# Feed-forward groups of a float32 decoder trunk: loads, sums, products and out units in another order

## The reference

```python
def _swiglu(x, w_in, w_out):
    gate, up = jnp.split(x @ w_in, 2, axis=-1)
    return (jax.nn.silu(gate) * up) @ w_out

x = x + 0.5 * _rmsnorm(_swiglu(_rmsnorm(x, ng[0]), ffn1_w_in[i], ffn1_w_out[i]), ng[1])
```

## Time and profile before

| | us |
|---|---|
| median of 3 runs | 2258.42 (2258.36 to 2259.06) |
| profiled execution | 2256.88 |
| its span, first to last instruction | 2255.2 |
| TensorE busy | 2199.7 (98%) |
| VectorE busy | 1549.6 (69%) |
| ScalarE busy | 1139.2 (51%) |
| GpSimd busy | 366.1 (16%) |

### The profile page before, as it was taken

How to read it: one execution, slowest core, us unless ns; L and a number is a source line. 1 busy time by engine, 2 the same in 40 slices (tenths; PEclk the granted TensorE clock), 3 DMA queues, 4 the chain that set the end, 5 groups by cost and what they waited for, 6 DMA issues and landing times.

```text
span 2255.2 us, 30953 instructions
## 1 busy us (share of the span) xinstructions
PE 2199.7 (98%) x11642; PEld 1819.9 (81%) x11642; DVE 1549.6 (69%) x1942; ACT 1139.2 (51%) x1639; POOL 366.1 (16%) x287
## 2 busy tenths in 40 slices
PE   9999999999999999999999999999999999999999
PEld 7788788788787887888787887787778888778787
DVE  6989536777568996358888338877666735888723
ACT  5445434655555455345445436567566734544422
POOL 2031000100111120001212001021822110121200
PEclk9999999999999999999999999999999999999999
DMA  5322332222223323333331332222212132532241
GB/s 169 124 82 78 108 96 86 83 78 85 65 90 112 112 75 91 96 94 107 117 113 52 97 95 88 85 75 66 66 48 85 57 94 72 143 131 94 92 133 66
DMA packets 84767, 208.59 MB, mean 92 GB/s; under 512 B 25088, under 2 KB 29312, under 8 KB 84640
## 3 DMA queue, kind: packets, MB, share of 16 engines
q1 hardware_dynamic: 84112, 206.59, 29.4%
q10 hardware_dynamic: 528, 0.26, 0.0%
HBM read 202.56 MB, written 4.26 MB: 92 GB/s over the span
## 4 chain that ended last, share of the span: by engine, by line
PE 78%; DVE 10%; issue 5%; ACT 3%; POOL 2%; DMA 2%; SPq 0%; DVEq 0%; ACTq 0%; POOLq 0%
PE bank L2514 37%; PE bank L2593 18%; PE bank L2941 9%; PE bank L2703 5%; DVE w_lo L1515 2%; DVE w_lo L1631 1%; PE bank L2668 1%; DMA raw_more<-in_ffn_in 1%; DVE h_lo L1520 1%; ACT w_hi L821 1%; ACT h_hi L833 1%; DVE resid L1550 1%; PE bank L3103 1%; PE bank L3082 1%; PE bank L3110 1%
## 5 line engine op out<-in xcount | busy, mean ns | idle before, releaser
L1515 DVE TENSOR_TENSOR w_lo<-raw,w_hi 128x1024 fp32r<-128x1024 f32 x283 | 360.0, 1284 | 427.8 <-ACT w_hi L821 427.2
L2593 PE MATMUL bank<-w_hi,factor 128*128 128x512 f32 x1792 | 553.8, 390 | 8.5 <-DVE w_lo L1631 4.6
L821 ACT ACTIVATE w_hi<-raw 128x1024 fp32r<-128x1024 f32 x283 | 293.8, 1054 | 277.3 <-PE bank L2514 191.1
L2593 PEld LDWEIGHTS bank<-w_hi,factor 128*128 128x128 f32 x1792 | 334.8, 188 | 80.3 <-issue 11.6
L2593 PE MATMUL bank<-w_lo,factor 128*128 128x512 f32 x896 | 348.8, 389 | 0.0
L2514 PE MATMUL bank<-h_hi,w_hi 128*128 128x512 f32 (+1 forms) x775 | 295.1, 381 | 8.7 <-DVE h_lo L1520 3.3
L2514 PE MATMUL bank<-h_hi,w_lo 128*128 128x512 f32 (+1 forms) x775 | 284.6, 367 | 0.0
L2514 PE MATMUL bank<-h_lo,w_hi 128*128 128x512 f32 (+1 forms) x748 | 274.5, 367 | 0.0
L2514 PE MATMUL bank<-act_late,w_hi 128*128 128x512 f32 (+1 forms) x648 | 200.7, 367 | 0.0
L2593 PEld LDWEIGHTS bank<-w_lo,factor 128*128 128x128 f32 x896 | 168.2, 188 | 35.2
L2514 PEld LDWEIGHTS bank<-h_hi,w_hi 128*128 128x128 f32 x775 | 146.1, 188 | 41.0 <-issue 10.3
(11 more groups left out here) (364 smaller groups left out, 3941.5 us busy)
## 6 DMA issues: line engine op xcount, KB each, us to landing
raw<-in_ffn_in SPq DMA_DIRECT2D x84, 512.0 KB, 3.7
raw<-in_gd_in SPq DMA_DIRECT2D x49, 512.0 KB, 3.7
raw_more<-in_ffn_in SPq DMA_DIRECT2D x48, 512.0 KB, 3.8
raw_last<-in_ffn_in SPq DMA_DIRECT2D x40, 512.0 KB, 4.8
raw<-in_ffn_out SPq DMA_DIRECT2D x48, 384.0 KB, 3.1
raw<-in_hg_in SPq DMA_DIRECT2D x32, 512.0 KB, 3.7
raw<-in_ffn_out SPq DMA_DIRECT2D x48, 320.0 KB, 2.9
raw<-in_last_out SPq DMA_DIRECT2D x22, 512.0 KB, 3.7
```

Of the source, the lines that this page charges most:

```text
L821: nc.scalar.activation(w_hi[:, u[0] % RING, :], raw[:, u[0] % RING, :], ACT.Copy).then_inc(hi_split, 1)
L1515: nc.vector.tensor_tensor(w_lo[:, r, :], raw[:, r, :], w_hi[:, r, :].bitcast(f32), ALU.subtract).then_inc(lo_split, 1)
L2593: ins = nc.tensor.matmul(bank[dst[t]][:], factor[:, 2 * i + ml, at:at + P], (w_hi, w_lo)[wl][:, u % RING, b * TOK:(b + 1) * TOK], start=st ...
```

## The change

Three parts, in all four feed-forwards:

1. The last plain unit is multiplied in two halves (chunks 0 to 3, then 4 to 7), and the first counts in `y_turned`. Turn 0's loads of half 0 of up and lower up wait for that, those of half 1 for the whole unit as before. In turn 0 VectorE takes step and join of half 0 first, then those of half 1 (`step_made` and `joined` give the new counts), and the sums and low halves behind them in another order.
2. Turn 0's early rows are multiplied by VectorE (`early_rows(0)`, in turn 1 behind the join's low halves) in place of GpSimd. `first_silu(1)` and `turn(0)` wait for VectorE's count instead.
3. At the end, ScalarE splits out units 0 and 1 ahead of the late silu and units 2 and 3 between it and the table load; VectorE splits unit 0 between `act_low(6)` and `act_low(7)`, unit 1 behind `late_gates`, unit 2 behind `early_ups`, unit 3 behind `act_low(13)`, and the early rows come last.

```diff
 FIRST = 2 * 16
-ACT_ROWS, DVE_ROWS, POOL_ROWS, TURNED = 45, 69, 20, 17
+def step_made(s, q, a):
+    return 8 * quad(s, q) + 1 + (a if q else 2 * a)
+def joined(s, q, a):
+    return 8 * quad(s, q) + (3 + a if q else 2 + 2 * a)
+ACT_ROWS, DVE_ROWS, POOL_ROWS, TURNED = 45, 71, 18, 18
...
-    return up_early(s, QUADS - 1, t) + 2
+def early_made(s, q, t):
+    return up_early(s, q, t) + 2
+def half_read(s):
+    return TURNED * ffn_no[s] + 1
...
+        def h_read(a):
+            if a == 0:
+                sp.wait_ge(y_turned, half_read(s))
+            else:
+                sp.wait_ge(unit_used, u0 + 2 * PLAIN)
         def up_quarter(q, a):
             if q == 0:
-                sp.wait_ge(unit_used, u0 + 2 * PLAIN)
+                h_read(a)
             else:
...
             if q == 0:
-                sp.wait_ge(unit_used, u0 + 2 * PLAIN)
+                h_read(a)
             else:
...
         def join_weights(q, a):
-            act.wait_ge(joint_made, 8 * quad(s, q) + 3 + a)
+            act.wait_ge(joint_made, joined(s, q, a))
             weights_high(q, 6, a, join_place(s, q, a))
...
         def step_weights(q, a):
-            act.wait_ge(joint_made, 8 * quad(s, q) + 1 + a)
+            act.wait_ge(joint_made, step_made(s, q, a))
             weights_high(q, 5, a, gate_place(s, q, a))
...
             for t in range(2):
-                if q:
+                if q > 1:
                     act.wait_ge(pool_rows, y_early(s, q - 1, t))
+                elif q:
+                    act.wait_ge(dve_rows, early_made(s, 0, t))
                 else:
...
         act_high(PLAIN + 7)
+        v0 = u0 + IN_UNITS["ffn"]
+        split((v0, 0))
+        split((v0 + 1, 0))
         late_silu(q)
+        split((v0 + 2, 0))
+        split((v0 + 3, 0))
         act.preload_act_table_set("natural_log_exp_and_others")
-        v0 = u0 + IN_UNITS["ffn"]
-        for n in range(RING):
-            split((v0 + n, 0))
         for f in range(4):
...
             dve.wait_ge(quarter_loaded[3][a], FIRST + 16 * (quad(s, q) + 1))
-            dve.wait_ge(joint_made, 8 * quad(s, q) + 1 + a)
+            dve.wait_ge(joint_made, step_made(s, q, a))
             TT(join_place(s, q, a), lower_up_place(s, q, a), gate_place(s, q, a), ALU.subtract).then_inc(joint_made, 1)
...
         def rest_sum(q, a):
-            dve.wait_ge(joint_made, 8 * quad(s, q) + 3 + a)
+            dve.wait_ge(joint_made, joined(s, q, a))
             TT(lower_gate_place(s, q, a), lower_gate_place(s, q, a), join_place(s, q, a), ALU.subtract).then_inc(joint_made, 1)
...
-        def last_rows():
+        def early_rows(q):
             for t in range(2):
-                dve.wait_ge(dve_rows, up_early(s, QUADS - 1, t))
-                dve.wait_ge(act_rows, silu_first(s, QUADS - 1, t))
+                dve.wait_ge(dve_rows, up_early(s, q, t))
+                dve.wait_ge(act_rows, silu_first(s, q, t))
                 TT(y_first[:, t, :], y_first[:, t, :], y[:, t, :], ALU.mult).then_inc(dve_rows, 1)
...
                 weights_low(q - 1, 3, 0, lower_up_place(s, q - 1, 0))
-            step_sum(q, 1)
+            if q:
+                step_sum(q, 1)
+            else:
+                join_sum(0, 0)
             if q:
...
                 late_gates(q - 1)
-            join_sum(q, 0)
             if q:
+                join_sum(q, 0)
                 weights_low(q, 2, 1, lower_gate_place(s, q, 1))
-            join_sum(q, 1)
-            weights_low(q, 6, 0, join_place(s, q, 0))
+                join_sum(q, 1)
+                weights_low(q, 6, 0, join_place(s, q, 0))
+                early_ups(q - 1)
+                weights_low(q, 6, 1, join_place(s, q, 1))
+                if q == 1:
+                    early_rows(0)
+                rest_sum(q, 0)
+                rest_sum(q, 1)
+            else:
+                step_sum(0, 1)
+                weights_low(0, 6, 0, join_place(s, 0, 0))
+                join_sum(0, 1)
+                factor_low(3)
+                weights_low(0, 6, 1, join_place(s, 0, 1))
+                rest_sum(0, 0)
+                weights_low(0, 5, 0, gate_place(s, 0, 0))
+                rest_sum(0, 1)
+            diff_sum(q, 0)
             if q:
-                early_ups(q - 1)
-            else:
-                factor_low(3)
-            weights_low(q, 6, 1, join_place(s, q, 1))
-            rest_sum(q, 0)
-            rest_sum(q, 1)
-            diff_sum(q, 0)
-            weights_low(q, 5, 0, gate_place(s, q, 0))
+                weights_low(q, 5, 0, gate_place(s, q, 0))
             diff_sum(q, 1)
...
         weights_low(q, 3, 1, lower_up_place(s, q, 1))
-        for k in range(PLAIN, PLAIN + 4):
+        v0 = u0 + IN_UNITS["ffn"]
+        act_low(PLAIN)
+        split((v0, 0))
+        act_low(PLAIN + 1)
+        late_gates(q)
+        split((v0 + 1, 0))
+        for k in range(PLAIN + 2, PLAIN + 6):
             act_low(k)
-        late_gates(q)
-        act_low(PLAIN + 4)
-        act_low(PLAIN + 5)
-        v0 = u0 + IN_UNITS["ffn"]
-        split((v0, 0))
+        early_ups(q)
+        split((v0 + 2, 0))
         act_low(PLAIN + 6)
         act_low(PLAIN + 7)
-        early_ups(q)
-        split((v0 + 1, 0))
-        last_rows()
-        split((v0 + 2, 0))
         split((v0 + 3, 0))
+        early_rows(q)
         for f in range(4):
...
                 late_product(q, t)
-            for t in range(2):
+            for t in range(2 if q else 0):
                 early_product(q, t)
...
                     blocks(bank[banks[q]][:], u, 5, (h_hi, h_lo), range(5, KD), False, True).then_inc(unit_used, 1)
+                elif i == PLAIN // 2 - 1 and q == RING - 1:
+                    blocks(bank[banks[q]][:], u, 0, (h_hi, h_lo), range(KD // 2), True, False).then_inc(y_turned, 1)
+                    blocks(bank[banks[q]][:], u, KD // 2, (h_hi, h_lo), range(KD // 2, KD), False, True).then_inc(unit_used, 1)
                 else:
...
             last = q == QUADS - 1
-            if last:
+            if last or q == 0:
                 pe.wait_ge(pool_rows, y_late(s, q, 1))
-                pe.wait_ge(dve_rows, last_early(s, 1))
+                pe.wait_ge(dve_rows, early_made(s, q, 1))
             else:
...
             for f in range(4):
```

More of the change, by code:

```diff
@@ L448, in join_made @@
         def join_made(s, q, t):
-            return DVE_ROWS * ffn_no[s] + 27 + 10 * q + t + 1
+            return DVE_ROWS * ffn_no[s] + 27 + 10 * q + (2 if q else 0) + t + 1
         def diff_added(s, q, t):
@@ L466, in y_late @@
         def y_late(s, q, t):
-            return POOL_ROWS * ffn_no[s] + PLAIN + 4 * q + t + 1
+            return POOL_ROWS * ffn_no[s] + PLAIN + 4 * q - (2 if q else 0) + t + 1
         def y_early(s, q, t):
             return y_late(s, q, t) + 2
-        def last_early(s, t):
-            return up_early(s, QUADS - 1, t) + 2
+        def early_made(s, q, t):
+            return up_early(s, q, t) + 2
+        def half_read(s):
+            return TURNED * ffn_no[s] + 1
         def first_halves(s):
-            return TURNED * ffn_no[s] + 1
+            return TURNED * ffn_no[s] + 2
         def turned_by(s, q, f):
-            return TURNED * ffn_no[s] + 1 + 4 * q + f + 1
+            return TURNED * ffn_no[s] + 2 + 4 * q + f + 1
         act_order = [*range(PLAIN), *range(KF - 8, KF - 4), *range(PLAIN, KF - 8), *range(KF - 4, KF)]
```

## The result

| | before | after |
|---|---|---|
| median, same chip, 20 runs each (us) | 2256.49 (2252.16 to 2259.90) | 2260.65 (2254.69 to 2266.41) |
| ratio after / before, 95% interval | | 1.0019 [1.0011, 1.0026] |
| profiled execution / its span (us) | 2256.88 / 2255.2 | 2256.96 / 2255.2 |

The change is slower by 0.2%, about the least that can be told from none. I had forecast 2242.2 and a range of 2237 to 2255. The profiled execution of after lies 3.7 us under its own median: its granted clock was 0.995, and over the 20 executions the time falls as that clock rises (0.990 at 2266.41, 0.9935 on average; 0.994 for the kernel before, in its runs beside the experiments). So the stages are compared in the two traces, which are equally long, and the verdict is left to the medians.

A forecast was written before the change was run, and what follows sets the result against it. TensorE, busy 98% of the span, was taken as the bound, so only its waits could pay. Gains of 2.4 (front), 4.5 (turn(0)) and 9.3 (tail), 16.2 us together, gave 2240.7 profiled and 2242.2 as median; range 2237 to 2255.

The forecast's parts named there:

- Between these ends I take the first: At turn(0): GpSimd's `up` gets in before 130.6, so TensorE waits for nothing; 4.5 us gained, hardly better than even.
- The other end: At turn(0): `up` runs only at turn 1's joins; TensorE waits 3.2 us in each of four, a loss of 8.3.
- thirteen quick `up` products: Of sixteen `up` products, those beside the three of 8.04 us took 2.0 each, behind one VectorE instruction at most.
- the two instructions of 0.60 that were to break the beat: VectorE's two early rows ahead of turn(0), expected to break the even rhythm in which `up` lost.
- fourth rival: At turn(0): GpSimd starves in all four and TensorE's clock goes to 0.50 behind each wait; 2261 us, chance 0.05.
- the second (0.24): GpSimd starves at every turn(0); 3.4 us saved, 2255.0, or 2257 with the low bound; chance 0.24.
- The front: Turn 0's loads and VectorE order: TensorE gains what VectorE gains, 0.6 us a feed-forward, 2.4 in all.
- step(0)'s wait: In the middle of step(0): a new TensorE wait of 1.4 us for the second low half, due at 94.6.
- the small one at turn 1: A small TensorE wait at turn 1's first product, whose low half is made at 104.5.
- The reason given: In turn 0 VectorE has 22.2 us of instructions in 23.04 and so bounds that stretch.
- The tail: Out units split ahead of the silus: 9.3 us gained, bounds 7.1 and 12.5, with up to 1.2 waited at turn(3).
- The range: Whole kernel, 2237 to 2255 us; lower end is the forecast with the tail's upper bound and half of step's wait.

The follow-up runs named there:

- part1: The kernel before with part 1 of the change alone; 2259.24 us, ratio 1.0017 to the kernel before.
- parts13: The changed kernel with turn 0's early rows back on GpSimd (parts 1 and 3 alone); 2251.88 us, ratio 0.9979 to the kernel before.
- late_tick2: The changed kernel with one short ScalarE copy, written to row_sum, ahead of each first late silu; 2261.81 us, ratio 1.0026 to the kernel before.
- high_ticks: The changed kernel with two short ScalarE copies ahead of the w_hi that VectorE's next instruction needs; 2262.54 us, ratio 1.0025 to the kernel before.
- late_ticks: The changed kernel with two short ScalarE copies, written to row_sum, ahead of each first late silu; 2261.61 us, ratio 1.0033 to the kernel before.
- front2: let_in with VectorE's turn 0 in another order; 2238.74 us, ratio 0.9923 to the kernel before.
- psum_window: The changed kernel with two unused VectorE sums that read PSUM ahead of early_rows(0); 2245.01 us, ratio 0.9950 to the kernel before.
- shifted: let_in with an unused one-column tile added, no instruction changed; 2269.98 us, ratio 1.0065 to the kernel before.
- let_in: The changed kernel with VectorE waiting for GpSimd's late products of turn 0 ahead of early_rows(0); 2246.48 us, ratio 0.9955 to the kernel before.
- part2: The kernel before with part 2 alone, turn 0's early rows on VectorE; 2261.72 us, ratio 1.0019 to the kernel before.
- part3: The kernel before with part 3 alone, the out units split ahead; 2249.07 us, ratio 0.9969 to the kernel before.
- before_tick: The kernel before with one short ScalarE copy ahead of each first late silu; 2254.32 us, ratio 0.9999 to the kernel before.
- before_high_ticks: The kernel before with two short ScalarE copies ahead of the w_hi that VectorE's next instruction needs; 2256.81 us, ratio 1.0005.

## Why the prediction was wrong

- **The step that failed** is "Between these ends I take the first", for `up` at turn(0): 4.5 us gained. The other end had been worked out at 3.2 us in each of four, 8.3 lost; 3.10 to 3.13 and 7.9 came. What spoke for the first end were thirteen quick `up` products, but twelve of the sixteen aren't at this place at all, and of the four that are, three had starved. And the two instructions of 0.60 that were to break the beat passed without GpSimd.
- **Part 1's side effect** was missed. The text let part 1 work on the front alone; part1, parts13 and after show all four turns starved with it. By which time it does so is open: two candidates fell.
- **The clock** behind the long waits was in the fourth rival, at all four. In after's trace it fell behind two, 1.6 us each. Three later kernels have the same waits of 3.1 us, and their traces show half clock behind four (late_tick2), four (high_ticks) and three (late_ticks). Two more in after's other executions would be 3.2 us, and its median lies 3.7 above its trace; that fits, but no trace of those executions is kept. The fourth rival's 2261 is what the median shows, for which I gave 0.05; the second (0.24) had the same mechanism without the clock, and came to 2255 to 2257. high_ticks, behind its four waits (columns as above):

```profile
135.00:138.30 3.30, 3.30 (x14) 2.99 (x13) 1.22 (x1) 2.74 (x5) 0.00 (x0) 0.50 0.27 106
770.00:773.00 3.00, 2.83 (x14) 2.86 (x15) 0.14 (x1) 1.45 (x3) 0.07 (x1) 0.50 0.55 190
1128.50:1131.50 3.00, 2.63 (x13) 2.66 (x14) 0.34 (x1) 1.25 (x3) 0.27 (x1) 0.50 0.77 214
2022.80:2025.80 3.00, 3.00 (x12) 2.71 (x12) 1.22 (x1) 2.60 (x5) 0.00 (x0) 0.50 0.19 75
```

- **The front** was right: 2.2 against 2.4, step(0)'s wait 1.24 against 1.4, the small one at turn 1 0.32. The reason given, that VectorE has no more to give there, was wrong: front2 took another 0.9 from each. So the right size was in part luck.
- **The tail** was right in kind and 1.4 too large: 7.9, between 7.1 and 9.3. In the first and third GpSimd got in twice, so turn(3) waits 1.27; in the second it was starved there too (4.55 and 5.91 us), which helps TensorE: 0.33. The last gave 1.6 for 2.2, its first low half of unit 2 being 3.1 us late.
- **The range**: by the terms that it names, its lower end comes to 2236.2, not 2237 (3.2 for the tail, 2.8 for half of step's wait). Nothing hangs on it.

## What to carry to other kernels

A GpSimd instruction on the critical path, beside a VectorE that runs without a gap, can be held up until VectorE's next stop or read of PSUM, 12.1 us here: look in the profile for one whose time varies (1.4, 2.3, 8.0, 12.1 us for one shape), and give it its place by a semaphore or by an instruction that reads PSUM. Filling VectorE's gaps, or moving work to it, can close the window that such an instruction lived by. When a bet between two ends hangs on one stretch, count the cases from that stretch alone.

## What the runs showed of the hardware

- GpSimd lost its memory to eleven VectorE instructions in a row, 12.1 us, at all sixteen turn(0) of after, late_tick2, late_ticks and high_ticks. In every trace it got in at the latest where VectorE next stood or began to read PSUM, as L1762 in psum_window; sometimes also between two that read SBUF alone (`gate` in after, asked for at 236.83, 2.14 us). Neither the instant of its request (0.07 to 0.11 us ahead lost, 0.08 to 0.10 ahead won) nor that of VectorE's operand decides.
- Moving tiles by one more column in front of them put the matmuls that read them 0.006 us further apart (0.233 for 0.227 at the median), 1% of the kernel (shifted against let_in).
- TensorE's granted clock went to half behind a wait of 3.1 us at turn(0) in 13 of 17 cases (after 2 of 4, late_ticks 3, late_tick2 and high_ticks 4 each, part2 0 of 1), and in none of the 17 where that wait was 1.5 to 1.6 us (before, part1, part3, parts13, before_tick, before_high_ticks). It also did in mixer stretches that no kernel touched, in some executions and not in others.
